# Expert scatter in a hybrid decoder trunk: one fp32 matmul with weighted selection against two fp32r matmuls with a one-hot selection

## The reference

```python
def moe_ffn(h, w_router, w_e_gate, w_e_up, w_e_down):
    logits = jnp.einsum('bsd,de->bse', h, w_router, preferred_element_type=jnp.float32)
    top_vals, top_idx = lax.top_k(logits, TOP_K)
    top_w = jax.nn.softmax(top_vals, axis=-1)
    combine = jnp.sum(jax.nn.one_hot(top_idx, N_EXPERTS, dtype=jnp.float32) * top_w[..., None], axis=-2)
    ...
    for e in range(N_EXPERTS):
        y = y + combine[..., e:e + 1] * swiglu(h, w_e_gate[e], w_e_up[e], w_e_down[e])
    return y
```

## Time and profile before

| | |
|---|---|
| three runs | 1180.06, 1178.82, 1178.95 us (median 1178.95) |
| the profiled execution | 1182.07 us |
| its span from first to last instruction | 1180.3 us |
| TensorE, VectorE, ScalarE busy | 94%, 71%, 57% of the span |
| routing | about 722 to 752 us of the span |
| the eight experts | about 752 to 1170 us |

### The profile page before, as it was taken

One profiled execution on the slowest core, in us unless ns is written; L12 is line 12 of the kernel. 1 busy time (PEld: TensorE's weight loads), 2 busy tenths in 40 slices (PEclk: granted clock), 3 DMA queues, 4 the chain that ended last, 5 costly groups with the idle time before them and its releaser, 6 DMA issues.

```text
span 1180.3 us, 16889 instructions
## 1 busy us (share of the span) xinstructions
PE 1106.9 (94%) x6535; PEld 946.1 (80%) x6535; DVE 837.0 (71%) x1124; ACT 672.1 (57%) x956; POOL 74.0 (6%) x119
## 2 busy tenths in 40 slices
PE   4999899997999998999899986899999999999997
PEld 3978677777999998989677875787888888887885
DVE  3577866775544545557867786588898888988885
ACT  3566555454434435457554544476677676777763
POOL 4001421000000000000512000000000000000000
PEclk9999899998999999999899997699999999999999
DMA  6553344556456545345244446389899899999992
GB/s 196 182 179 116 108 143 143 172 179 220 153 169 226 185 140 170 98 144 179 81 143 143 144 157 234 97 300 365 273 340 346 310 332 308 379 311 361 327 330 94
DMA packets 147670, 250.19 MB, mean 212 GB/s; under 512 B 5166, under 2 KB 108676, under 8 KB 147588
## 3 DMA queue, kind: packets, MB, share of 16 engines
q1 hardware_dynamic: 145808, 246.89, 62.1%
q10 hardware_dynamic: 1780, 2.19, 0.6%
HBM read 248.02 MB, written 1.05 MB: 211 GB/s over the span
## 4 chain that ended last, share of the span: by engine, by line
PE 78%; DVE 14%; ACT 4%; issue 2%; POOL 1%; DMA 1%; ACTq 0%; DVEq 0%; POOLq 0%
PE PS L622 24%; PE PS L1077 9%; PE PS L1078 9%; PE PS L1079 9%; PE PS L938 5%; PE PS L940 5%; PE PS L939 5%; DVE w_lo L402 4%; DVE m_lo L1756 3%; PE PS L1048 2%; PE PS L710 2%; PE PS L648 1%; PE PS L1036 1%; ACT w_hi L393 1%; DVE small L1898 1%
## 5 line engine op out<-in xcount | busy, mean ns | idle before, releaser
L402 DVE TENSOR_TENSOR w_lo<-ring,w_hi 128x1536 fp32r<-128x1536 f32 (+1 forms) x192 | 311.7, 1634 | 126.9 <-ACT w_hi L393 126.3
L393 ACT ACTIVATE w_hi<-ring 128x1536 fp32r<-128x1536 f32 (+1 forms) x192 | 264.7, 1388 | 153.0 <-PE PS L940 86.3
L1756 DVE TENSOR_TENSOR m_lo<-ring,m_hi 128x512 fp32r<-128x512 f32 (+2 forms) x256 | 185.9, 755 | 89.5 <-ACT m_hi L1275 87.8
L1275 ACT ACTIVATE m_hi<-ring 128x512 fp32r<-128x512 f32 (+2 forms) x256 | 157.1, 630 | 140.0 <-PE PS L622 137.6
L1077 PE MATMUL PS<-w_hi,hTe 128*96 128x384 f32 (+1 forms) x384 | 131.5, 342 | 0.7 <-issue 0.7
L622 PE MATMUL PS<-m_hi,h_hi 128*128 128x512 f32 (+2 forms) x352 | 127.1, 361 | 3.2 <-DVE m_lo L1756 2.6
L1078 PE MATMUL PS<-w_hi,hTe 128*96 128x384 f32 (+1 forms) x384 | 124.5, 324 | 0.0
L1079 PE MATMUL PS<-w_lo,hTe 128*96 128x384 f32 (+1 forms) x384 | 124.4, 324 | 0.0
L622 PE MATMUL PS<-m_hi,h_lo 128*128 128x512 f32 (+2 forms) x352 | 121.8, 346 | 0.0
L622 PE MATMUL PS<-m_lo,h_hi 128*128 128x512 f32 (+2 forms) x352 | 121.8, 346 | 0.0
L938 PE MATMUL PS<-h_hi,w_hi 128*128 128x256 f32 x352 | 100.8, 286 | 0.8 <-DVE h_lo L1738 0.8
(11 more groups left out here) (320 smaller groups left out, 2213.4 us busy)
## 6 DMA issues: line engine op xcount, KB each, us to landing
ring<-in_w_in_dram SPq DMA_DIRECT2D x40, 1024.0 KB, 5.3
ring<-in_w_exp_gate_dram SPq DMA_DIRECT2D x24, 1536.0 KB, 7.6
ring<-in_w_exp_up_dram SPq DMA_DIRECT2D x24, 1536.0 KB, 9.4
ring<-in_w_exp_down_dram SPq DMA_DIRECT2D x24, 1536.0 KB, 8.6
ring<-in_w_branch_dram SPq DMA_DIRECT2D x12, 1024.0 KB, 5.0
ring<-in_w_ffn_gate_dram SPq DMA_DIRECT2D x6, 1536.0 KB, 6.6
ring<-in_w_ffn_up_dram SPq DMA_DIRECT2D x6, 1536.0 KB, 7.3
ring<-in_w_ffn_down_dram SPq DMA_DIRECT2D x6, 1536.0 KB, 6.7
```

The source lines that it names most:

```text
L393: act.activation(split_parts(u, j)[0], ring[:, i % NSLOT, w0:w0 + words], ACT.Copy)\
L402: dve.tensor_tensor(lo, ring[:, (j // 2) % NSLOT, w0:w0 + words], hi.bitcast(F32), SUB).then_inc(sem(f"lo_ready{b}"), 1)
L1275: act.activation(hi, raw, ACT.Copy).then_inc(sem("m_hi_ready"), 1)
L1756: dve.tensor_tensor(lo, raw, hi.bitcast(F32), SUB).then_inc(sem("m_lo_ready"), 1)
```

## The change

`wsel` is gone. `selT` becomes the transpose of the bare one-hot `psel`, held in fp32r. `rows_out` splits the result of an expert: ACT copies both column halves into `ye_hi` (fp32r), and DVE subtracts both from PSUM into `ye_lo`, each behind ACT's copy of the same half. `scatter` runs two fp32r matmuls for each chunk, `selT` by `ye_hi` and `selT` by `ye_lo`. The weights come in `added`: a SCALAR_TENSOR_TENSOR multiplies the chunk by `wt` of its token, a scalar per partition, and adds `x_tok`. `weigh` moves on DVE from between `psel` and the first gathers to between experts 0 and 1; only its maximum (now `most_rows`) stays where it was.

```diff
-                pe.wait_ge(sem("ye_act"), n + 1)
-                pe.wait_ge(sem("ye_dve"), n + 1)
+                pe.wait_ge(sem("ye_lo_ready"), 2 * n + 2)
...
-                    pe.matmul(PS[:, 4 + b, :], selT[:, e, a * P:(a + 1) * P], ye[:, d * 512:(d + 1) * 512],
-                              start=True, stop=True).then_inc(sem(f"aux_full{b}"), 1)
+                    rows, w = selT[0:CAP, e, a * P:(a + 1) * P], slice(d * 512, (d + 1) * 512)
+                    pe.matmul(PS[:, 4 + b, :], rows, ye_hi[0:CAP, w], start=True, stop=False)
+                    pe.matmul(PS[:, 4 + b, :], rows, ye_lo[0:CAP, w], start=False, stop=True).then_inc(sem(f"aux_full{b}"), 1)
...
             def prepare(r, part):
-                pe.wait_ge(sem("sel_ready"), 2 * (r + 1))
...
-                                              wsel[:, a, 2 * c + i, :], ident[:, :])
+                                              psel[:, a, 2 * c + i, :].bitcast(F32), ident[:, :])
...
-                            pe.wait_ge(sem("ye_act"), n)
-                            pe.wait_ge(sem("ye_dve"), n)
+                            pe.wait_ge(sem("ye_lo_ready"), 2 * n)
...
-                act.activation(ye[:, 0:512], PS[0:CAP, 6, :], ACT.Copy).then_inc(sem("ye_act"), 1)
+                for c in range(2):
+                    act.activation(ye_hi[0:CAP, c * 512:(c + 1) * 512], PS[0:CAP, 6 + c, :], ACT.Copy).then_inc(sem("ye_hi_ready"), 1)
...
-                wait_used(dve, expert_unit(n), HALVES - 1)
-                dve.tensor_copy(ye[:, 512:1024], PS[0:CAP, 7, :]).then_inc(sem("ye_dve"), 1)
+                for c in range(2):
+                    w = slice(c * 512, (c + 1) * 512)
+                    dve.wait_ge(sem("ye_hi_ready"), 2 * n + c + 1)
+                    dve.tensor_tensor(ye_lo[0:CAP, w], PS[0:CAP, 6 + c, :], ye_hi[0:CAP, w].bitcast(F32), SUB)\
+                       .then_inc(sem("ye_lo_ready"), 1)
...
-                    dve.tensor_tensor(x, x, PS[:, 4 + b, :], ADD).then_inc(sem(f"aux_free{b}"), 1)
+                    dve.scalar_tensor_tensor(x, PS[:, 4 + b, :], wt[:, a, e - 1:e], x, MUL, ADD).then_inc(sem(f"aux_free{b}"), 1)
...
+            def most_rows():
+
+                step(dve.tensor_reduce(rsm[:, 8:9], PS[:, 1, TT * NE:(TT + 1) * NE], AX.X, MAX))
...
-                step(dve.tensor_reduce(rsm[:, 8:9], PS[:, 1, TT * NE:(TT + 1) * NE], AX.X, MAX))
...
                 if isinstance(r, int):
-                    weigh()
+                    most_rows()
                 dve.wait_ge(sem("psel_ready"), 2 * (r + 1))
-                for a in range(TT):
-                    dve.tensor_tensor(wsel[:, a], psel[:, a].bitcast(F32), wt[:, a, :].unsqueeze(2).broadcast_to([P, NE, CAP]), MUL)\
-                       .then_inc(sem("sel_ready"), 1)
...
                 for e in range(NE):
+                    if e == 1 and isinstance(r, int):
+                        weigh()
                     expert(r, e, n + e)
```

More of the change, by code:

```diff
@@ L217, in hybrid_trunk @@
         ropes = sb("ropes", [P, DEPTH, 2, 2, TT, ROPE])
-        htok_lo, = over(("htok_lo", [P, TT, D], F32R))
+        htok_lo, ye_hi, ye_lo = over(("htok_lo", [P, TT, D], F32R), ("ye_hi", [P, D], F32R), ("ye_lo", [P, D], F32R))
         big = sb("big", [P, 24 * T])
@@ L260, in hybrid_trunk @@
         y_parts = {0: (yA_hi, yA_lo), 2: (yB_hi, yB_lo), 1: (yA_hi, yA_lo)}
-        psel, = over(("psel", [P, TT, NE, CAP], F32R))
+        psel, _, selT = over(("psel", [P, TT, NE, CAP], F32R), ("qk_mid", [P, 512], F32), ("selT", [P, NE, T], F32R))
         qk = sb("qk", [P, 4096])
@@ L300, in hybrid_trunk @@
         hidf = big[:, 5120:5120 + 3 * T].rearrange("p (f t) -> p f t", f=3)
-        selT = qk[0:CAP, 2048:2048 + NE * T].rearrange("p (e t) -> p e t", e=NE)
-        wsel = big[:, 2048:2048 + TT * NE * CAP].rearrange("p (a e c) -> p a e c", a=TT, e=NE)
-        ye = big[0:CAP, 3584:3584 + D]
         sile = big[0:CAP, 4608:4608 + 2 * GB].rearrange("p (f t) -> p f t", f=2)
@@ L1608, in expert @@
                                 wait_aux_full(act, b, uses)
-                                act.activation(selT[:, 2 * c:2 * c + 2, :], two(PS[0:CAP, 4 + b, :]), ACT.Copy)\
+                                act.activation(selT[0:CAP, 2 * c:2 * c + 2, :], two(PS[0:CAP, 4 + b, :]), ACT.Copy)\
                                    .then_inc(sem(f"aux_free{b}"), 1)
```

## The result

The changed kernel took 1173.14 us (median of 8 runs, 1172.06 to 1176.54) against 1180.46 us before (8 runs). The ratio is 0.994 with a 95% interval of 0.9925 to 0.9955. So the change is faster, by 0.45 to 0.75%, or 7.1 us by the ratio. Forecast were 10.5 us, and 1173.14 lies 0.14 us above the range. The profiled execution took 1175.41 us with a span of 1173.7; before it was 1182.07 and 1180.3.

What follows compares the result with a forecast made beforehand. PE was taken to set the pace, DVE and transfers close behind. Routing 2.0, expert 1 0.3, experts 2 to 7 8.4, end -0.2 make 10.5 us: 1168.4 us, range 1165.0 to 1173.0.

Steps and rivals of the forecast that it cites:

- the scatter's matmuls: Experts 1 to 7: fp32r steps of 0.23 us make a part 0.92 instead of 1.72 us, 11.2 us at most.
- an fp32r pair that is no cheaper (4): Scatter: fp32r pair costs as much as fp32, 0.43 us a step, parts give nothing: 1177.3 us, chance 0.04.
- a slow subtraction (5): Row split on DVE: subtractions held up in PSUM; with 1.7 us each about 1182 us, chance 0.03.
- DVE's costs: In each expert: subtractions in front of half 3 add 0.61 us, each weighted add 0.06 us.
- the price of `weigh`: In front of expert 1: `weigh` takes 2.1 us, makes DVE 1.1 us late; expert 1 gains only 0.3 us.
- Rival 2: DVE takes more, each new instruction 0.1 us: 6 to 8 us gained in all, 1171 to 1173 us, chance 0.10.
- the bank waits: Scatter's part 1: PE waits 0.05 then 0.2 us for DVE's adds to free aux banks, 0.23 us an expert.
- rival 1: Everything on DVE hides, expert 1 without loss: 12.5 to 13 us gained, 1166 us, chance 0.12.
- I cost it at nothing: Expert weight loads: the tightest has 1.0 us to spare, so late loads cost nothing.
- rival 3: The loads bind: at 339 GB/s experts stay at 51 us, only the routing gains: about 1177.2 us, chance 0.05.
- the routing: Gathers and expert 0 start 2.0 us earlier, worth 2.0 us; 1.0 if the clock's rise stays, 2.7 if earlier.
- the end: Behind expert 7: PE starts 1.2 us later, chunks are shorter, net +0.2 us, bounds 0 and +0.6.

Runs made afterwards that it cites:

- split_only: The changed kernel with the selection again multiplied by token weights, the plain add, and `weigh` back in front of the gathers: 1173.28 us.
- weigh_early: The changed kernel with `weigh` moved in front of expert 0, behind the first copies of gathered tokens: 1173.43 us.
- adds_first: The changed kernel with the two adds of the scatter's part 0 put ahead of the product of group 0 on DVE: 1171.41 us.
- part1_later: The changed kernel with part 1 of the scatter and its adds one half later, behind half 5: 1172.39 us.
- light_loads: The changed kernel with loads D2 and D3 of every expert cut to half their columns, the other half stale: 1172.81 us.
- weights_only: The kernel before with only the bare selection, the weighted add and the moved `weigh`, the scatter still fp32: 1180.66 us.
- warm_long: The changed kernel with 16 matmuls of zeros in one unbroken row behind the router: 1172.42 us.
- stay_warm: The changed kernel with matmuls of zeros in PE's waits from the end of layer 1's mixer to the first gather: 1167.58 us.
- warm_routing: The changed kernel with 6 matmuls of zeros between router and ranking and 5 between ranking and first gather: 1173.98 us.

## Why the prediction was off

**Right: what bounds the kernel, and the scatter's matmuls.** A step is 0.23 us and a part without waits 0.92, in the chain of expert 2 (866.30 to 867.21), so the sum by steps of 0.131 us is out. The wait at half 20 kept its size, as argued (PE's step there is 0.71 us before, 0.72 after). `split_only` alone has the whole gain. The rivals of an fp32r pair that is no cheaper (4) and of a slow subtraction (5) are refuted: 679 ns.

**Right: DVE's costs, and nearly the price of `weigh`.** The weighted add takes 0.741 us (0.74 forecast), the steps of the subtraction are 0.60 (0.61), `weigh` 2.1. Rival 2 had 6 to 8 us in all, which is what was measured, but by costs of DVE's instructions that did not come, so its number fits by luck. Expert 1 gained 0.30 us, 0.3 forecast. But the reckoning said that `weigh` took 1.1 us of it, and `weigh_early` gave back 0.9. PE's step to part 1 of expert 1 is 1.07 us where 0.17 is the step without a wait, so it waits 0.9 us there, for the "over 1 us" forecast.

**Wrong in size: the bank waits, 0.23 us forecast, 0.37 to 0.39 measured.** The step is "With a signal's 0.05 us it waits 0.05 and then another 0.2". The banks came free when forecast, so rival 1, in which everything hides, falls. But PE's weight load for a chunk stood behind the same wait and could no longer be done during the matmul ahead. So a bank that is free just in time still costs 0.1 to 0.2 us: in expert 2 the steps around the first chunk are 0.35 for 0.17 and 0.31 for 0.23, around the second 0.26 and 0.34 for 0.23. Over six experts that is 0.9 us. `adds_first` and `part1_later`, in which these steps are gone, show the cause.

**Wrong for this execution: "I cost it at nothing", for the loads.** I checked one load, the one with the least time to spare, by a single landing time. In the changed kernel the late ones were the up loads behind it, the one in the chain with 11.20 us to landing. They took 1.0 us in the profiled execution, which is how the sum of the stages has them. How much of it is in the median of the eight runs is not shown. `light_loads` and the other profiles show that it is no pace: rival 3 is refuted as a mechanism, and the residue varies.

**Wrong in size: the routing, 2.0 forecast, 1.04 measured.** Gathers and expert 0's start moved by 1.98 us, as worked out. The failing step is the choice "I take 2.0" between 1.0 and 2.7: the clock rose where it had risen before, and the lower bound was the answer. `weights_only` shows the same (0.95). The Trainium skill's rule in "TensorE: Matmul & The Clock Gate", Part 1: The HAM clock gate, that sustained activity lifts the clock, is borne out by `warm_long` (a rise in its row of 16) and `stay_warm`. Closing the gap of 1.8 us between gathers did not bring the rise forward (28.4 us behind the router's first matmul for 28.3), nor did the 11 matmuls of `warm_routing` (27.7, and 34.1 behind the fall like the others).

**Wrong in size: the end, +0.2 forecast, +0.72 measured.** The later start (+1.2) was right. "The last add starts at 1174.4 to 1174.6" took the full clock for granted. PE idled for 2.0 us behind expert 7 and for 0.5 between the parts, and its clock fell before the last two chunks. The steps of 0.43 instead of 0.23 cost 0.5 us: the last add started 0.83 us later than before, and in `adds_first`, where the clock stayed up, 0.30 later, the upper end of the forecast.

The four misses, 1.0 us for the clock in the routing, 0.9 for the bank waits, 1.0 for the loads and 0.5 for the end, plus 0.2 from rounding 1.37 up to 1.4, make 3.6: the difference between 10.5 and 6.86 us, in which the loads stand as this one execution has them. All four lay on the same side: each of my values near nothing had a cost. The 6.86 us of the stages agree with the 7.1 of the ratio (5.3 to 8.9 by its interval). What moves the part ahead of the router from one execution to the next was not tried.

## What to carry to other kernels

When an engine on the path gets faster, go through every place where it meets another engine and compare the time to spare with the time saved. Count a wait that ends just in time as up to 0.2 us for a lost early weight load, and expect what you free in one place to be asked for at the next. Work that is moved forward into a stretch at the low clock is worth half. Look there first: 42 matmuls of zeros in PE's waits gave 5 to 6 us here, nearly as much as the change. Take the time at single stages when the effect is smaller than the spread of the runs.

## What had not been expected of the hardware

- Matmuls of zeros by zeros (bf16, 512 columns) bring PE's clock up: 16 in a row raised it from 0.50 before they had ended, 5.80 us in all; 6 and 5 with other work between them did not. In PE's wait for `psel` the clock fell in `warm_long` and did not in `stay_warm`, which has 9 of them there.
- The router's records of 8 columns, in which PE is busy for 6.9 us of 728 to 735 in the changed kernel, ran with the clock at 0.50 in every kernel that has no matmuls of zeros ahead of them. In `stay_warm` the clock was at 1.00 when they began and fell 0.9 us into them. So the clock was low here, and even fell, while PE was busy by its records.
- The same instructions ahead of the router ended between 726.4 and 731.7 us in profiles of kernels that are equal there. Differences of 1 or 2 us in a single span tell nothing here.
